# A transformer forward pass on one core: a quarter of the first expert stage's tiles as three rounded products, scores moved into the query stage, shorter pair sums, and VectorE's order by an estimated clock

## The reference

```python
def one_chunk(xc):                                   # h (256, 1024) in two chunks of 128 tokens
    q = (xc @ w_q).reshape(t, 8, 2, 128)             # 16 half queries per token
    sc = jnp.einsum('thpc,hpnc->thpn', q, sub_keys)  # 128 scores per half query
    v_half, i_half = lax.top_k(sc, 16)
    cand = v_half[:, :, 0, :, None] + v_half[:, :, 1, None, :]      # 16 x 16 pair sums per head
    top_s, pos = lax.top_k(cand.reshape(t, 8, -1), 16)
    expert = ...                                     # 16 of 16384 experts per head
    g = jax.nn.softmax(top_s, axis=-1)
    act = gelu(jnp.einsum('thkd,td->thk', u_tab[expert], xc))
    return jnp.einsum('thk,thkd->td', g * act, v_tab[expert])
```

## Time and profile before

| | us |
|---|---|
| median of 3 runs | 2076.83 (2076.51 to 2081.11) |
| the profiled execution | 2068.39 |
| its span, first to last instruction | 2066.6 |
| mean granted TensorE clock | 0.992 of full speed |

### The profile page before, as it was taken

How to read it: one execution, slowest core, us unless ns; L and a number is a source line. 1 busy time by engine, 2 the same in 40 slices (tenths; PEclk the granted TensorE clock), 3 DMA queues, 4 the chain that set the end, 5 groups by cost and what they waited for, 6 DMA issues and landing times.

```text
span 2066.6 us, 35237 instructions
## 1 busy us (share of the span) xinstructions
PE 2007.3 (97%) x12408; PEld 1791.5 (87%) x12408; DVE 1622.2 (78%) x3208; ACT 857.9 (42%) x1653; POOL 385.0 (19%) x262
## 2 busy tenths in 40 slices
PE   8999999999999999999999999999999999999998
PEld 6888887779999999977887887899999998778786
DVE  6899886865799276699999967639964756999997
ACT  6557454545101100055565666531101002555665
POOL 0000000000024233303243100000352322232440
PEclk9999999999999999999999999999999999999999
DMA  6554344415389989867799853335998988678995
GB/s 258 198 203 163 114 139 156 138 67 174 133 337 341 368 321 327 300 241 229 262 351 356 294 184 117 113 117 195 391 353 309 346 306 317 224 243 281 371 377 181
DMA packets 132634, 511.17 MB, mean 247 GB/s; under 512 B 15004, under 2 KB 15132, under 8 KB 129856
## 3 DMA queue, kind: packets, MB, share of 16 engines
q1 hardware_dynamic: 95680, 375.81, 51.7%
q0 software_dynamic: 36864, 134.23, 17.6%
HBM read 508.94 MB, written 1.05 MB: 247 GB/s over the span
## 4 chain that ended last, share of the span: by engine, by line
PE 64%; DVE 16%; DMA 5%; issue 2%; ACT 2%; SPq 0%; DVEq 0%; ACTq 0%
PE bank L2383 30%; PE bank L344 8%; PE bank L346 8%; PE bank L345 8%; DVE tile_lo L2705 5%; DMA wbuf<-in_peer_v 3%; PE bank L2413 3%; PE bank L2414 3%; DVE x_tok L2258 2%; DMA wbuf<-in_peer_u 2%; PE bank L2282 1%; DVE w_parts L2708 1%; DVE e_hot_first L2274 1%; DVE e_hidden L2290 1%; DVE tile_lo L274 1%
## 5 line engine op out<-in xcount | busy, mean ns | idle before, releaser
L2383 PE MATMUL bank<-h_dense,wbuf 128*128 128x192 f32 x4096 | 679.7, 327 | 3.7 <-ACT e_stage L2467 2.4
L2383 PEld LDWEIGHTS bank<-h_dense,wbuf 128*128 128x128 f32 x4096 | 664.2, 190 | 6.0 <-issue 4.9
L2512 ACT ACTIVATE tile_hi<-wbuf 128x1024 fp32r<-128x1024 f32 x248 | 263.0, 1060 | 246.1 <-DMA wbuf<-in_peer_v 202.3
L2705 DVE TENSOR_TENSOR tile_lo<-wbuf,tile_hi 128x1024 fp32r<-128x1024 f32 x256 | 311.0, 1215 | 37.7 <-ACT tile_hi L2512 27.4
L2244 POOL DMA_INDIRECT e_gbuf<-in_peer_v,e_row_at x128 | 227.1, 1774 | 484.3 <-DVE x_tok L2258 445.8
L2494 ACT ACTIVATE e_hidden<-bank 128x384 f32<-128x384 f32 x128 | 62.7, 490 | 603.2 <-PE bank L2383 603.2
L2244 POOL DMA_INDIRECT e_gbuf<-in_peer_rows,e_row_at x128 | 155.8, 1218 | 470.1 <-DVE e_dots L2252 239.0
L2413 PE MATMUL bank<-tile_hi,w_parts 128*128 128x512 f32 x512 | 208.5, 407 | 11.1 <-DVE w_parts L2708 10.4
L274 DVE TENSOR_TENSOR tile_lo<-wbuf,tile_hi 128x1024 fp32r<-128x1024 f32 (+2 forms) x117 | 140.3, 1212 | 80.1 <-ACT tile_hi L266 79.2
L2414 PE MATMUL bank<-tile_lo,w_parts 128*128 128x512 f32 x512 | 200.4, 391 | 0.0
L344 PE MATMUL bank<-tile_hi,w_parts 128*128 128x512 f32 x512 | 200.1, 391 | 0.0
(11 more groups left out here) (391 smaller groups left out, 3500.3 us busy)
## 6 DMA issues: line engine op xcount, KB each, us to landing
wbuf<-in_peer_u SPq DMA_DIRECT2D x256, 512.0 KB, 5.7
wbuf<-in_peer_v SPq DMA_DIRECT2D x256, 512.0 KB, 5.0
wbuf<-in_w_in SPq DMA_DIRECT2D x16, 2048.0 KB, 7.7
wbuf<-in_peer_q SPq DMA_DIRECT2D x32, 512.0 KB, 3.8
wbuf<-in_hyb_in SPq DMA_DIRECT2D x16, 512.0 KB, 3.7
wbuf<-in_mla_uq SPq DMA_DIRECT2D x9, 512.0 KB, 3.4
wbuf<-in_mla_in SPq DMA_DIRECT2D x8, 528.0 KB, 4.2
wbuf<-in_w_v SPq DMA_DIRECT2D x2, 2048.0 KB, 7.3
```

The costliest lines, as they stand in the source:

```text
L2383: last = nc.tensor.matmul(bank[:, j // 2 % 2, j % 2 * S:j % 2 * S + DENSE], ring[:, slot, k * P:(k + 1) * P], h_dense[:, k, :], start=(k = ...
L2512: nc.scalar.activation(tile_hi[:, slot, 0:D], ring[:, slot, 0:D], ACT.Copy).then_inc(hi_done, 1)
L2705: nc.vector.tensor_tensor(tile_lo[:, slot, 0:D], ring[:, slot, 0:D], tile_hi[:, slot, 0:D].bitcast(F32), ALU.subtract).then_inc(lo_done, 1)
```

## The change

In the U stage every fourth tile of rounds 1 to 14, that is 28 of 128 tiles (`MIXED`), is computed as `three_products`: 24 fp32r matmuls with 192 columns in place of 8 plain ones. For it ScalarE rounds the tile (`rounded_u`, after the Gelu of a pair), VectorE forms its rest (`mixed_rest`), and `h` is split once into parts. The slot of such a tile is freed by `tile_lo`; loads are issued in the order 0, 3, 1, 2 of each four. The scores of each pair of query tiles are issued inside the query stage, and VectorE searches the first 12 half queries of one token block there too. The 16 x 16 pair sums become 17 rows of 8 (136 in place of 256 per head). The turned transposes take all 128 rows of both token blocks. VectorE's order in the U stage comes from an estimated time `now`: `passes` places each `mixed_rest` and each item when its due time has come. By that planner 76 items are taken by the end of U. No item is taken in the weighing part of V any more; the other 52 are spread over tiles 56 to 116. `hidden` is split for two tiles at once (`pair_rounded` on ScalarE, after the rounding of the second tile of the pair; one VectorE subtraction per pair). `acts` gets its Gelu in two parts, and the clearing of `x[LOW]` moves from GpSimd to VectorE.

```diff
+    MIXED = 2 * (ROUNDS - 2)
+    HI_0, LO_0 = M_U + NKEYS - MIXED, M_U + NKEYS - MIXED
+    IN_FOURS = [j + e for j in range(0, STEP, SLOTS) for e in (0, 3, 1, 2)]
+    def load_first(sp):
+        def used_slot(r, j):
+            sp.wait_ge(used, STEP * r + M_U + j - SLOTS + 1)
+            load_slot(sp, U, STEP * r + j, (M_U + j) % SLOTS)
+        def rested_slot(r, j):
+            sp.wait_ge(lo_done, 2 * r + LO_0 + j // SLOTS - 2)
+            load_slot(sp, U, STEP * r + j, (M_U + j) % SLOTS)
...
-    TAKEN, LAST_TAKE = (16, 30, 36, 78, 88), 116
-    EXPS_AT, ACTS_AT = (16, 30), 54
+    EXPS_AT, ACTS_AT, ACTS = (14, 32), (50, 61), (slice(0, 48), slice(48, SHARED))
+    ROWS_1 = PK + 1
+    PAIR, LAST_TAKE = 5.02, 116
+    ROW_AT = (42.0, 3.4, 36, 192.0, 3.4)
...
         def dense_turned(out, source):
-            nc.tensor.transpose(out[:, 0:LATE], source(slice(0, LATE), 1), ident[0:LATE, 0:LATE])
-            return nc.tensor.transpose(out[:, LATE:DENSE], source(slice(0, P), 0), ident)
+            nc.tensor.transpose(out[:, 0:P], source(1), ident)
+            return nc.tensor.transpose(out[:, LATE:DENSE], source(0), ident)
...
+        def scores(pair):
+            pe.wait_ge(q_kept, pair + 1)
+            if pair >= 2:
+                for n in range(2):
+                    pe.wait_ge(sc_kept[n], pair - 1)
+            for t in range(NT):
+                for j in (2 * pair, 2 * pair + 1):
+                    last = nc.tensor.matmul(bank[:, 6 + pair % 2, ...], q_T[:, j, ...], keys[:, j, :], start=True, stop=True)
+            last.then_inc(sc_done, 1)
...
+        def mixed_experts(q, width, base, j):
+            slot = (M_U + j) % SLOTS
+            pe.wait_ge(lo_done, width // SLOTS * q + LO_0 + (base + j) // SLOTS - 1)
+            for k in range(KT):
+                last = three_products(nc, bank[:, j // 2 % 2, S:S + DENSE], tile_hi[:, slot, :], tile_lo[:, slot, :],
+                                      h_part(h_parts_hi, k), h_part(h_parts_lo, k), k, k == 0, k == KT - 1)
+            last.then_inc(used, 1)
...
-            pe.wait_ge(w_lo_done, width * q + base + j + 1)
+            pe.wait_ge(w_lo_done, width // 2 * q + (base + j) // 2 + 1)
...
-        def hidden_rounded(a, slot):
-            part = hidden[:, bass.ds(a, 1), :].rearrange("p a t -> p (a t)")
-            nc.scalar.activation(w_parts[:, slot, LATE + DENSE:LATE + 2 * DENSE], part, ACT.Copy).then_inc(w_hi_done, 1)
-            nc.scalar.activation(w_parts[:, slot, 0:LATE], part[:, 0:LATE], ACT.Copy).then_inc(w_hi_done, 1)
+        def pair_rounded(a, slot):
+            part, slots = hidden[:, bass.ds(a, 2), :], slice(slot, slot + 2)
+            nc.scalar.activation(w_parts[:, slots, LATE + DENSE:LATE + 2 * DENSE], part, ACT.Copy).then_inc(w_hi_done, 1)
+            nc.scalar.activation(w_parts[:, slots, 0:LATE], part[:, :, 0:LATE], ACT.Copy).then_inc(w_hi_done, 1)
...
             nc.scalar.activation(tile_hi[:, slot, 0:D], ring[:, slot, 0:D], ACT.Copy).then_inc(hi_done, 1)
-            hidden_rounded(STEP * r + j + SLOTS, j % SLOTS)
+            if j % 2:
+                pair_rounded(STEP * r + j + SLOTS - 1, (j - 1) % SLOTS)
...
+        def passes(spent):
+            nonlocal now
+            now += spent
+            while rested < MIXED and now >= (STEP // 2 + 2 * rested + 1) * PAIR - 3.0:
+                mixed_rest()
+                now += 1.22
+            while rows_known and taken < ITEMS and now >= (ROW_AT[0] + taken * ROW_AT[1] if taken < ROW_AT[2] else ROW_AT[3] + (taken - ROW_AT[2]) * ROW_AT[4]):
+                take()
+                now += 1.27
...
         for n in range(NGROUP):
             if n < NGROUP - 1:
                 one_hots(dve, 0, n + 1)
+                passes(1.95)
+            until((tile + 1) * PAIR / 2 + 0.45 * n + 3.0)
             weigh(dve, 0, n)
-            take(TAKEN[2] + (n + 1) * (TAKEN[3] - TAKEN[2]) // NGROUP)
+            passes(0.7)
+        until(NKEYS * PAIR / 2 + 0.45 * NGROUP - 6.0)
 
         def value_rest(a):
             slot, part = (M_V + a) % SLOTS, a % SLOTS
             dve.wait_ge(hi_done, a + M_V + 1)
             nc.vector.tensor_tensor(tile_lo[:, slot, 0:D], ...).then_inc(lo_done, 1)
-            dve.wait_ge(w_hi_done, 2 * a + 2)
-            hi, lo = (w_parts[:, part, b:b + DENSE] for b in (LATE + DENSE, LATE))
-            nc.vector.tensor_tensor(lo, hidden[:, a, :], hi.bitcast(F32), ALU.subtract).then_inc(w_lo_done, 1)
+            if a % 2 == 0:
+                dve.wait_ge(w_hi_done, a + 2)
+                hi, lo = (w_parts[:, part:part + 2, b:b + DENSE] for b in (LATE + DENSE, LATE))
+                nc.vector.tensor_tensor(lo, hidden[:, a:a + 2, :], hi.bitcast(F32), ALU.subtract).then_inc(w_lo_done, 1)
...
-            if a < WEIGHING * STEP:
-                take(TAKEN[3] + (a + 1) * (TAKEN[4] - TAKEN[3]) // (WEIGHING * STEP))
-            else:
-                take(TAKEN[4] + (a + 1 - WEIGHING * STEP) * (ITEMS - TAKEN[4]) // (LAST_TAKE - WEIGHING * STEP))
+            if a >= WEIGHING * STEP:
+                behind = ITEMS - before if a >= LAST_TAKE else (a + 1 - WEIGHING * STEP) * (ITEMS - before) // (LAST_TAKE - WEIGHING * STEP)
+                while taken < before + behind:
+                    take()
```

More of the change, by code:

```diff
@@ L2358, in tensor @@
                 turn_normed(4)
+            if j == 3:
+                pe.wait_ge(keys_loaded, DMA)
+            if j >= 3 and j % 2:
+                scores((j - 3) // 2)
         pe.wait_ge(h_done, KT)
         seed(0, P)
[L2361 to L2366, removed]
-                    pe.wait_ge(sc_kept[j // 4 % 2], j // 8 + 1)
-                last = nc.tensor.matmul(bank[:, j // 4, (j % 4) * P:(j % 4 + 1) * P], q_T[:, j, t * P:(t + 1) * P],
-                                        keys[:, j, :], start=True, stop=True)
-                if j % 4 == 3:
-                    last.then_inc(sc_done, 1)
+        scores(HALVES // 2 - 1)
         pe.sem_inc(weighted, 2)
-        for n in range(2):
-            pe.wait_ge(sc_kept[n], 4)
         def experts(q, width, base, j):
@@ L2458, in scalar @@
                 dense_columns(4)
+            if j == 5:
+                act.wait_ge(ns["rstd_step"], 4)
+            if j >= 5 and j % 2:
+                early_scores((j - 5) // 2)
             if j % 2:
@@ L2643, in vector, with take @@
         by_half = ((LOW, slice(0, SHARED)), (HIGH, slice(SHARED, PICKS)))
-        taken = 0
-        def take(upto):
+        taken, rested, now, rows_known = 0, 0, 0.0, False
+        def take():
             nonlocal taken
-            while taken < min(upto, ITEMS):
-                if taken == SHARED:
-                    dve.wait_ge(exps_done, NT + 1)
+            for n, part in enumerate(ACTS):
+                if taken == SHARED + part.start:
+                    dve.wait_ge(exps_done, NT + n + 1)
@@ L2664, in vector, with mixed_rest @@
-        find_picks(1, lambda: None)
+                    nc.vector.tensor_tensor(acts[:, part], acts[:, part], share[:, part], ALU.mult).then_inc(share_done, 1)
+                    dve.wait_ge(share_done, 3 + n)
+            if taken == SHARED:
+                dve.wait_ge(rows_zero, 1)
+            if taken < SHARED:
+                row_dot(dve, taken)
+            else:
+                row_value(dve, taken - SHARED)
+            taken += 1
+        def mixed_rest():
+            nonlocal rested
+            slot = (M_U + SLOTS - 1) % SLOTS
+            dve.wait_ge(hi_done, HI_0 + rested + 1)
+            nc.vector.tensor_tensor(tile_lo[:, slot, 0:D], ring[:, slot, 0:D], tile_hi[:, slot, 0:D].bitcast(F32), ALU.subtract).then_inc(lo_done, 1)
+            rested += 1
@@ new lines, in passes, with until @@
+        def passes(spent):
[7 more added lines that the diff above has]
+                now += 1.27
+        def until(when):
+            nonlocal now
+            while now < when:
+                passes(0.25)
@@ new lines, in vector @@
+        quiet = lambda spent: None
+        for j in range(HALVES):
+            if j >= 5 and j % 2:
+                late_scores(dve, (j - 5) // 2)
+            if j + SLOTS < HALVES:
+                rest_tile(nc, dve, g, M_Q + j + SLOTS)
+            if j >= 5 and j % 2:
+                dve.wait_ge(sc_kept[1], (j - 3) // 2)
+                best_halves(1, (j - 5, j - 4), 2, quiet)
+        dve.wait_ge(lo_done, M_U)
+        dve.sem_inc(lo_done, NKEYS - MIXED)
+        for pair in (HALVES // 2 - 2, HALVES // 2 - 1):
+            late_scores(dve, pair)
@@ L2665, in vector @@
+        dve.wait_ge(sc_kept[1], HALVES // 2)
+        best_halves(1, range(HALVES - 4, HALVES), 4, quiet)
+        now = 12.0
+        find_picks(1, passes)
         for rows, part in by_half:
```

293 lines of the change are left out of this document (173 added, 120 removed).

## The result

The changed kernel is slower: 2152.12 us median (2143.57 to 2158.40, 4 runs) against 2078.97 (2076.51 to 2086.41, 4 runs), ratio 1.0333, 95% interval 1.0293 to 1.0373. "No change" was wrong, and the time lies 48 us above the range. The profiled executions have spans of 2066.6 and 2152.3 us, 85.7 apart; the medians are only 73 apart, since the profiled execution of the kernel before was 8 to 11 us shorter than its medians and that of the changed kernel 2 longer. What follows adds up the difference of those two executions.

A forecast was written before the change was run, and what follows sets the result against it. U was taken as TensorE's alone, V as three engines and the DMA within 10% of each other. Terms -20.4 + 2 + 0.8 - 5.7 + 22 = -1.3 us on the profiled 2068.39, with medians 8.4 above: 2075.5 us, range 2056 to 2104.

The forecast's parts named there:

- No change: Whole kernel, the forecast case: rest of V at 2.54 to 2.68 us per tile, -8 to +6 us, chance 0.34.
- Mixed tiles: U stage: 192-column fp32r matmuls take 0.093 us, a mixed tile 2.24 us, -20.4 us for both layers.
- The rival with the floor: U stage: weight loading floors the mixed matmul at 0.112 us, -20.4 becomes +4.8, 2100 us in all; chance 0.12.
- a line through two widths: U stage: straight line through fp32r matmuls of 512 and 256 columns, giving 0.093 us at 192 columns.
- Stalls in U: U stage: late mixed rests and waits for loads cost +1 us per layer (0 to 5), +2 us.
- Mixed rests issued early: U stage, VectorE: due times omit weight groups, so towards tile 116 `mixed_rest` is issued some 11 us before its tile can be rounded.
- Edges of U: Around U: last copy shorter, -0.3 us per layer; 11 small transposes become full, +0.7; together +0.8 us for both.
- Weighing part: V's weighing part: without items and with one subtraction per pair TensorE's 5.14 us binds; -5.7 us, bounds 0 and -7.5.
- The rest of V: V after the weighing part: 52 items and the pair's wait give 2.6 us per tile, +9.3 and +12.7, together +22 us.
- the loop over landing + 4.7 us: Rest of V: a ring slot's loop takes load landing L + 4.7 us for four tiles; L = 6.7 gives 2.85 per tile.
- the landing of 5.6 us: Rest of V: load landing taken between rows of 7.2 and 4.7 us, giving 2.6 us per tile.
- the rest of V waits for loads: Rest of V: more gathers keep landing at 6 to 7 us, 2.68 to 2.85 per tile, +6 to +24 us; chance 0.22.

The follow-up runs named there:

- the edges' run: Changed kernel with the four loads at the U ring's second and last rounds issued in the order their slots come free: 2140.78 us, ratio 1.0287.
- the next run: Changed kernel with natural load order at both edges and the first item planned for 54.0 us, not 42.0, then one each 3.2 us: 2124.73 us, ratio 1.0272.
- the kernel with more items: Changed kernel, mixed tiles kept, natural load order at edges, hidden split per tile, 86 items ahead of V's rest: 2130.65 us, ratio 1.0285.
- the width run: Only matmuls, 48 of each width, fp32r and plain float32, no kernel around them: fp32r 0.111 us each at 224, 192 and 128 columns, 0.120 at 256.

## Why the prediction was wrong

- **Mixed tiles, 0.093 us a matmul, -20.4 us: failed.** It is 0.111, so 2.68 us a tile and +4 us for both layers. The rival with the floor had the mechanism and the size (0.112), and I gave it 0.12. The working had the decisive row in hand, 0.11 us at 64 plain columns. Weighed against it was a line through two widths that both lie above the bend; a line can't show a floor below its points.
- **Stalls in U, +2 us: failed, and by most.** U lost 51 us, 4 of them the floor; 6.5 stay without mixed tiles. I compared the median landing with the slot's time, in the middle of the stage. The stalls sit at the ends and at one event: the load order at the first and last group (18 us with the clock, by the edges' run), VectorE standing for the first gather (18 us, by the next run, with the edges already mended). None of the rivals held this. The median of a ring says nothing of the rounds in which its order of issue differs.
- **The clock.** Not a term of the sum. Gaps of 2 to 6 us brought 17 us at the lower level into the first layer's U stage, which before had none until its last matmul.
- **Mixed rests issued early, 11 us towards tile 116: right as a mechanism, too small and too late in the stage.** VectorE stood 83 us in the first layer, at 24 of the 28 rests; behind it TensorE waited 1.7 us, and 19.2 in the kernel with more items.
- **Edges of U, +0.8 us.** Small as forecast: what comes before the first U stage took 1.4 us more, what lies between the layers 3.0 less.
- **Weighing part, -5.7 us: right mechanism, more than the bound of -7.5.** It was -8.8, TensorE alone as forecast, and the clock dip that I let stay in the first layer did not come.
- **From U to V.** Not in the sum: 3.1 us won in the first layer.
- **The rest of V, +22 us: right mechanism, wrong size.** +48. The two parts were right by themselves: VectorE's own work, 2.44 us per tile with a split per tile, measured 2.46 without the pair, and the loop over landing + 4.7 us holds the pace with it. 2.85 us per tile is a landing of 4 x 2.85 - 4.7 = 6.7 us by that loop, and in the trace the rounding of tiles 72 to 103 starts 6.7 and 6.5 us (medians) after the issue of their loads. What failed is the landing of 5.6 us, the middle of two short windows. Over the same 32 tiles the kernel before has had 6.7 and 6.4 us all along (issues of loads in both layers: count, size, median landing in us):

```profile
wbuf<-in_peer_v SPq DMA_DIRECT2D x32, 512.0 KB, 6.7
...
wbuf<-in_peer_v SPq DMA_DIRECT2D x32, 512.0 KB, 6.4
```

  So loads did not land later than before; the pair put the same landing into a longer loop. The rival "the rest of V waits for loads" had 6 to 7. With 376 GB/s as the DMA's limit I also had a wrong reason for moderation: without the pair they moved 398.
- **Sum.** +4 (floor), +47 (stalls and clock in U), -3 (U to V), -9 (weighing), +48 (rest of V) make +87, of which other stages gave 1.7 back. That is the difference of the two profiled executions; by the medians it is 73. Of the first U stage's 27.2 us some 4 are not assigned to a place: its waits are 13 us more than before, the clock cost 7, the floor 2.

Two rivals came true together, and a third loss that was none of them came on top. Each was costed as if the others were absent.

## What to carry to other kernels

With 128 new weight columns each, a float32 or fp32r matmul record took 0.111 us here even where its columns alone would take less: count instructions times the larger of the two, and look for the floor in rows narrower than the one you plan, not on a line through wider ones. Before an operation is batched over two tiles, ask which is the later input of the batch and what stands behind it in an in-order queue; here moving one subtraction behind the odd tile's rest returned most of the loss in one stage and cost 7 us per layer in another. An order written by an estimated clock has to count all work of the pacing engine and must be read at its edges, the first event that is not yet ready and the last round.

## What the runs showed of the hardware

- In the width run, the 48 fp32r matmuls of 64 columns took 8.2 us against 5.5 for 128. The first 22 or so start 0.11 us apart, at 2.4 GHz; then the granted clock falls to 1.2 GHz, with TensorE issuing without a gap, and they start 0.213 apart. Plain float32 at 64 columns, two records each, kept 1.00 and took as long as at 128. The windows of 128 and of 64 columns in fp32r (the clock is the mean of the stretch):

```profile
56.27:61.60 5.33, 5.33 (x51) 5.33 (x49) 0.00 (x0) 0.00 (x0) 0.00 (x0) 1.00 0.01 3
61.60:69.56 7.96, 7.96 (x50) 7.96 (x50) 0.00 (x0) 0.00 (x0) 0.00 (x0) 0.65 0.00 0
```

- The DMA engines moved 398 to 403 GB/s over 78 us in the rest of V with the split per tile, and 350 over 91 us with the pair, at a busy share of 0.95: a share near 1 was not the limit that it looked like in the kernel before.
